# Gate matmuls of a two-layer hybrid encoder issued in two pieces, the first of them one attention item earlier

## What is computed

```python
h = _rms(x, p['norm_mix'])
(fq, fk, fv, fg, bq, bk, bv, iq, ik, iw, cqa, ckva, ckpe) = jnp.split(h @ p['w_in'], ...)
ya = ...  # forgetting attention (FoX), 6 heads
yb = ...  # attention over the keys that an indexer picks (DSA), 4 heads
yc = ...  # latent attention (MLA), 6 heads
g = jax.nn.sigmoid((h @ p['w_gate']).astype(f32)).astype(x.dtype)
ga, gb, gc = jnp.split(g, 3, axis=-1)
x = x + (ga * ya + gb * yb + gc * yc) @ p['w_o']
```

## Time and profile before

| what | us |
|---|---|
| runs, median (lowest to highest) of 3 | 2279.78 (2279.63 to 2280.76) |
| the profiled execution | 2279.32 |
| its span, first to last instruction | 2277.5 |
| PE busy in the span | 2200.3 (97%) |
| DVE, ACT, POOL busy | 1380.9, 1028.2, 392.2 |
| granted TensorE clock, mean | 0.995 |

### The profile page before, as it was taken

How to read it: one execution, slowest core, us unless ns; L and a number is a source line. 1 busy time by engine, 2 the same in 40 slices (tenths; PEclk the granted TensorE clock), 3 DMA queues, 4 the chain that set the end, 5 groups by cost and what they waited for, 6 DMA issues and landing times.

```text
span 2277.5 us, 37822 instructions
## 1 busy us (share of the span) xinstructions
PE 2200.3 (97%) x14028; PEld 1930.5 (85%) x14028; DVE 1380.9 (61%) x2738; ACT 1028.2 (45%) x2209; POOL 392.2 (17%) x282
## 2 busy tenths in 40 slices
PE   7999999999999999999999999999999999999999
PEld 7987767777888989989899877677778889899897
DVE  3546755545656946938545476555357489388393
ACT  4245666666625423424232456666566254133241
POOL 1110020120002504314012100201100034143140
PEclk9999999999999999999999999999999999999999
DMA  6232213205132222222232322131232222222222
GB/s 207 78 108 82 79 59 103 81 29 169 56 113 83 84 84 74 94 74 85 81 126 78 96 91 86 53 112 60 56 142 93 93 81 87 75 83 84 84 84 83
DMA packets 101397, 203.29 MB, mean 89 GB/s; under 512 B 36960, under 2 KB 58592, under 8 KB 101088
## 3 DMA queue, kind: packets, MB, share of 16 engines
q1 hardware_dynamic: 101216, 200.88, 26.9%
HBM read 176.89 MB, written 23.95 MB: 88 GB/s over the span
## 4 chain that ended last, share of the span: by engine, by line
PE 89%; ACT 4%; DVE 3%; issue 2%; POOL 1%; DVEq 1%; DMA 1%; SPq 0%; ACTq 0%
PE ps L806 26%; PE ps L846 15%; PE ps L1263 7%; PE ps L1262 7%; PE ps L1264 7%; PE ps L855 6%; PE ps L901 3%; PE ps L992 2%; PE ps L1009 2%; PE ps L920 1%; PE ps L946 1%; PE ps L960 1%; PE ps L1072 1%; PE ps L1052 1%; PE ps L965 1%
## 5 line engine op out<-in xcount | busy, mean ns | idle before, releaser
L1323 ACT ACTIVATE w_hi<-raw 128x1024 fp32r<-128x1024 f32 (+4 forms) x172 | 171.2, 998 | 421.2 <-PE ps L806 368.8
L1818 DVE TENSOR_TENSOR w_lo<-raw,w_hi 128x1024 fp32r<-128x1024 f32 (+4 forms) x124 | 139.0, 1123 | 205.2 <-ACT w_hi L1323 201.7
L846 PE MATMUL ps<-h_hi,w_hi 128*128 128x320 f32 x768 | 247.6, 322 | 1.4 <-ACT g L1323 1.4
L846 PE MATMUL ps<-h_hi,w_lo 128*128 128x320 f32 x768 | 237.4, 309 | 0.0
L846 PE MATMUL ps<-h_lo,w_hi 128*128 128x320 f32 x768 | 237.3, 309 | 0.0
L1765 POOL TENSOR_TENSOR rsq<-ssq,mhalf 128x12 f32<-128x12 f32 (+3 forms) x56 | 118.9, 2123 | 553.1 <-DVE ssq L1891 455.4
L1262 PE MATMUL ps<-th_hi,op_hi 128*128 128x320 f32 x640 | 198.0, 309 | 4.5 <-issue 4.5
L1264 PE MATMUL ps<-th_hi,op_lo 128*128 128x320 f32 x640 | 198.3, 310 | 0.0
L1263 PE MATMUL ps<-th_lo,op_hi 128*128 128x320 f32 x640 | 198.3, 310 | 0.0
L806 PE MATMUL ps<-w_hi,act_hi 128*128 128x512 f32 x440 | 173.9, 395 | 0.0
L806 PE MATMUL ps<-w_lo,act_hi 128*128 128x512 f32 x440 | 173.9, 395 | 0.0
(11 more groups left out here) (359 smaller groups left out, 5530.4 us busy)
## 6 DMA issues: line engine op xcount, KB each, us to landing
raw<-in_weights SPq DMA_DIRECT2D x212, 512.0 KB, 3.3
gates<-gst SPq DMA_DIRECT2D x72, 160.0 KB, 1.8
g<-gates SPq DMA_DIRECT2D x12, 960.0 KB, 6.9
raw<-in_weights SPq DMA_DIRECT2D x24, 384.0 KB, 3.1
kc<-in_cache_fox_k SPq DMA_DIRECT2D x16, 384.0 KB, 3.1
vc<-in_cache_fox_v SPq DMA_DIRECT2D x16, 384.0 KB, 3.7
x_sb<-in_x_prompt SPq DMA_DIRECT2D x8, 512.0 KB, 4.3
out_y_prompt<-x_sb SPq DMA_DIRECT2D x8, 512.0 KB, 3.4
```

The source lines that it names most:

```text
L846: mm = pe.matmul(ps[:, 5, 0:HALF], w[:, kk * P:(kk + 1) * P], h_pair[x][:, kk, half * HALF:(half + 1) * HALF], start=kk == 0 and n == 0, s ...
L1323: return act.activation(dst, src, ACT.Copy, scale=scale)
L1818: dve.tensor_tensor(low[:, 0:width], raw[raw_slot(c)][:, 0:width], high[:, 0:width].bitcast(F32), ALU.subtract).then_inc(lo_made.sem, 1)
```

## The change

A new table, `GATE_FROM[k]`, gives the step in which half k begins: one before `GATE_AT[k]`, if the half before it stands at least two steps earlier; else the same. For 35 of the 48 halves of a layer it is one step earlier: 7 to 17, 18, 19, 20 to 29, 31, 33, 34, 35, 37, 39, 40, 42 and 44 to 47. Of these, `gate_half(k, (0,))` issues contraction steps 0 to 3 (12 matmuls) at the end of step `GATE_FROM[k]`, after all of that step's work, and `gate_half(k, (1,))` issues steps 4 to 7 at the end of step `GATE_AT[k]`. The other 13 are issued whole, as before. Both pieces carry the waits for `lo_made` and `g_moved`; only the second raises the semaphore. The tables of ACT, DVE and SP are the same as before.

```diff
+GATE_FROM = [_n - (_n > GATE_AT[_k - 1] + 1) if _n >= 0 else _n for _k, _n in enumerate(GATE_AT)]
+GATES_BEGUN = [[_k for _k in range(GATE_HALVES) if GATE_FROM[_k] == _n < GATE_AT[_k]] for _n in range(N_ITEMS + 6)]
...
-                def gate_half(k):
+                def gate_half(k, parts=(0, 1)):
...
-                    for kk in range(KD):
+                    for kk in range(4 * parts[0], 4 * parts[-1] + 4):
                         for n, (w, x) in enumerate(w_of(C_GATE + m)):
                             mm = pe.matmul(ps[:, 5, 0:HALF], w[:, kk * P:(kk + 1) * P], h_pair[x][:, kk, half * HALF:(half + 1) * HALF],
                                            start=kk == 0 and n == 0, stop=kk == KD - 1 and n == 2)
-                    mm.then_inc((g_done, w_used)[half].sem, 1)
+                    if parts[-1]:
+                        mm.then_inc((g_done, w_used)[half].sem, 1)
...
                     for k in GATES_IN[step]:
-                        gate_half(k)
+                        gate_half(k, (1,) if GATE_FROM[k] < step else (0, 1))
+                    for k in GATES_BEGUN[step]:
+                        gate_half(k, (0,))
```

## The result

| kernel | median, us | lowest to highest |
|---|---|---|
| before | 2279.78 | 2279.63 to 2280.76 |
| after | 2289.47 | 2289.01 to 2291.20 |

The ratio is 1.0041, 95% interval 1.0030 to 1.0053: slower by 9.7 us, where 6.5 were predicted; the forecast's own range was 2283 to 2291. The profiled execution of the changed kernel took 2290.46 us, with a span of 2288.7, 11.2 more than before. The same matmuls run, yet PE's busy time is 4 us more; I take that for the filling and draining of the array, which rows that follow closely hide in each other; no run here tests it. First the page's line of busy times, then its row for the first of the three gate products (busy and mean ns, then the idle time before it and who ended it). In the kernel before that last figure was 1.4 us.

A forecast was written before the change was run, and what follows sets the result against it. PE, busy 97% of the span, was taken as the bound. Layer 0: 6.7 + 1.1 + 0.6 + 0.3 - 5.6 = +3.1 us, layer 1 +3.4, together +6.5, giving 2286.3 us; range 2280.0 to 2293.0.

The forecast's parts named there:

- The fixed part: Fox items, halves 7 to 17: first pieces wait for ACT's copy of the half before, 6.7 us in a layer.
- The signs named beforehand: Right: fox pieces start 0.7 to 0.8 us after the half before, layer 0's items 2 to 5 us longer, five brackets gone.
- signs of being wrong: Fox `gst` copy over 0.2 us late, fox under 4 us longer, mlas shorter, or mla pieces waiting for `g_moved`.
- rival 2: Fox items: ACT comes late to the gate copy and PE waits, 5 us more a layer, 2296 us; chance 0.13.
- rival 1: Bank wait only as brackets say, fox 3.8 us, mlas gives 1.6: -2.2 us a layer, 2275.7 us; chance 0.27.
- on time by 0.1 us at halves 8 and 9: Fox items: ACT reaches the gate copies in time, by 0.1 us at these halves and by more elsewhere.
- The 1.03 us at 364.47: Values of item 30, behind half 20's first piece: their wait for a cache load goes, 1.03 us; 0.75 in layer 1.
- Half 42: Dsa items: its first piece costs 0.46 us behind half 41; the turn's wait at 537.22, bracket 0.56 us, goes.
- The mla turns: Mla items: three turns that wait for ACT now stand behind a piece, gaining 0.15 to 0.2 us each, 0.5 us.
- the +0.3 that was chosen: Mlas items, around half 31's first piece: a cost of 0.3 us, within bounds of -1.6 and +1 us.

The follow-up runs named there:

- The longer copy: Changed kernel, with ACT copying halves 6 to 16 out of bank 5 in ten pieces of 32 columns: 2302.63 us, ratio 1.0105 against the kernel before.
- covering the wait: Changed kernel, with first pieces of halves 7 to 17 right behind the scores and masks of the half's own step: 2276.69 us, ratio 0.9989 against the kernel before.
- The run with six and two steps: Changed kernel with pieces of six and two contraction steps instead of four and four: 2318.01 us, ratio 1.0176 against the kernel before.
- The kernel with the chosen pieces: Changed kernel, but only halves 20 to 29, 35, 39, 44 and 47 in two pieces: 2270.86 us, ratio 0.9958 against the kernel before.

## Why the prediction came out as it did

**Sign and mechanism: right.** The pieces of the fox items wait for `gst`, 0.78 us from end to start, and the change is slower. The fixed part was sized at 6.3 us a layer (with the 0.35 that one piece gives back) and measured at 6.25 where nothing else disturbs it. The longer copy adds its length eleven times, and covering the wait takes the loss away.

**The signs named beforehand.** Those of being right came, with two exceptions: the pieces of halves 8, 9 and 10 began 1.15, 0.88 and 0.96 us after the end of the half before and not 0.7 to 0.8, and layer 0's items grew by 5.8 us and not by 2 to 5. Two signs of being wrong came in small: `gst` copies that begin later than 0.2 us (behind halves 7, 8, 9 and 17; rival 2), and mlas shorter, by 0.1 to 0.2 us (rival 1).

**Size: 9.7 instead of 6.5 us.** Four terms, in us of the profiled execution, both layers:

- **ACT's lateness, +1.4 in fox and +1.1 at step 23.** The text had it "on time by 0.1 us at halves 8 and 9". It was 0.4 late behind half 7 and 0.2 behind halves 8 and 9, with a wait of 0.23 us for DVE ahead of the copy. Step 23 was not looked at: half 17 has no piece close behind it, so I counted no cost. Its second piece still hurries ACT, and `ct` is behind the copy in ACT's queue.
- **The wait that moved, +2.2.** The 1.03 us at 364.47 did go. But its neighbour at 361.77, which stands before the piece and waited 0.60 us for the same kind of load, grew to 1.91. A first piece covers only what stands behind it; the load's own time is a row that I had not read. This term is partly chance, as the landing times show.
- **Half 42, +0.7.** Its turn no longer waits, as predicted, but the second piece ends early, ACT copies late, and half 43 in the next step starts 1.05 us behind instead of 0.69. It is rival 2 again at a place where I had only looked for the first piece's wait.
- **The others: within 0.5 us each a layer.** Halves 35, 37, 39, 44, 45, 46 and 47 gave -1.08, +0.60, -0.21, -0.71, +0.30, +0.28 and -0.74; the prediction had -0.95, +0.65, -0.34, -0.84, +0.3, +0.3 and -0.8. The mla turns gave 0.63 where 0.5 stood. In mlas the piece took 0.84 off at one step and the next gave 0.94 back; the later steps returned 0.28, so the stage came out at -0.18 in layer 0: inside the bounds, but on the other side of nothing than the +0.3 that was chosen.

Added to the predicted 6.5 the first three make 11.9, and the others return 0.8. That is 11.1, the sum of the table (5.77 + 5.38) and the difference of the profiled executions (2290.46 - 2279.32). That of after lay 1.0 us above its median, that of before 0.5 below, hence 9.7. So by the traces the miss is 4.6 us and not 3.2; that the medians lie nearer to the forecast is no merit of its terms.

**Rival 1** had the bank wait at the brackets' size, 3.8 us in fox. The bracket reads 0.51 for half 12 where the shift is 0.75: it counts from the modelled end of the matmul before. **Rival 2** had a mechanism that is there, at a quarter of its full size: 2.5 of the 10 us it named, or 3.2 with half 43. The run with six and two steps shows how near it was; 0.88 us less cover made it the larger price.

## What to carry to other kernels

- A piece moved up to fill waits must be asked two things: what it waits for where it now stands, and who has less time because the rest of the work ends sooner. The second can be answered only by following ACT's queue behind the second piece; here it was followed, and came out 0.3 us too early at halves 8 and 9.
- Where one PSUM bank serves a chain of groups, put enough PE work between a group's end and the next one's start to cover the copy: 0.2 us until it starts, 0.44 for the copy and 0.05 to 0.14 until PE goes on. A second bank for the gates would be another way to take the wait out; no run here tried it.
- Measure such a table of placements piece by piece from the starts in the trace, and keep the pieces that gain: the single costs added up to within 1 us here.

## What the chip showed that was not expected

**A wait of 2 us was followed by the slow clock.** In the run with six and two steps, `ct` came so late that PE stood still for 1.97 us. PE's row there, and windows of four us (busy us of PE, PEld, DVE, ACT, POOL, then the granted clock):

```profile
300.40 0.98 PE L905 MATMUL ps<-consts,kc 128*128 128x128 f32 x6 [1.97 <-ACT ct L1329]
```

```profile
296.00:300.00 4.00, 2.43 (x18) 1.89 (x18) 2.11 (x6) 3.72 (x9) 0.00 (x0) 1.00 0.05 13
300.00:304.00 4.00, 3.60 (x22) 2.17 (x22) 2.94 (x6) 3.13 (x8) 0.00 (x0) 0.62 0.09 32
304.00:308.00 4.00, 4.00 (x11) 2.77 (x10) 0.55 (x1) 0.71 (x2) 0.00 (x0) 0.52 0.71 231
308.00:312.00 4.00, 3.84 (x29) 2.25 (x28) 2.05 (x9) 2.46 (x6) 0.42 (x1) 1.00 0.01 4
```

PE was busy for 2.43 of the 4 us before, then ran at 0.52 to 0.62 of full clock, the lower of its two levels (1.2 GHz) for most of the 8 us, and the next scores came 2.9 us later than they would have. The other layer has the same at the same step (3.1 us), and with two smaller ones (1.6 at the end of the foxs items, 1.4 in mlas of layer 1) that makes 9.0 of the 28.5 us of that run. The one in mlas came at a wait of 2.32 us; its twin of 2.31 us in layer 0 was followed by full clock. A wait of that length is not needed either. The kernel with the chosen pieces had one such stretch at a place with no piece nearby: 1.6 us in layer 1 of its profiled execution, at 0.72 of full clock between 1482 and 1486 us, behind waits of 0.27 and 0.38 us. That of the kernel before with the copy in ten pieces (its windows stand above) came behind waits of 0.89 and 0.76 us for the cache loads, while the kernel before had 0.60 and 1.03 there and kept full clock. So a wait can cost more than its length, but not every time, and what decides it is open; a difference of 1.6 us between two profiled executions can be this alone.

**Small copies are dear in sum.** Ten copies of 32 columns took 1.0 us where one of 320 took 0.44, about 0.06 us more for each of the nine further ones.
